# Gated linear attention: one stage written out in place of a loop over heads

## The reference

```python
h = x @ w_in                       # q, k (4 x 256), v, z (4 x 512), a (16)
g = log_sigmoid(a @ w_a2 + b_a) / 16
G = cumsum(g, axis=2)              # within chunks of 64 tokens
G_last = G[:, :, -1:]
q_t = q * 256 ** -0.5 * exp(G)
k_t = k * exp(-G)
k_s = k * exp(G_last - G)
A = where(tril, q_t k_t^T, 0)
o = A v + (what the chunks before left in the state S, through q_t)
o = o * rsqrt(mean(o * o) + eps)   # per head, over its 512 values
y = (o * gn_g * silu(z)) @ w_out
```

## Time and profile before

| what | us |
|---|---|
| median of 3 executions | 1978.28 |
| lowest and highest | 1973.71 and 1978.42 |
| profiled execution, its own time | 1979.1 |
| its span, first to last instruction | 1977.2 |
| mean granted TensorE clock | 0.945 of full |

### The profile page before, as it was taken

One profiled execution on the slowest core, in us unless ns is written; L12 is line 12 of the kernel. 1 busy time (PEld: TensorE's weight loads), 2 busy tenths in 40 slices (PEclk: granted clock), 3 DMA queues, 4 the chain that ended last, 5 costly groups with the idle time before them and its releaser, 6 DMA issues.

```text
span 1977.2 us, 23196 instructions
## 1 busy us (share of the span) xinstructions
PE 1782.6 (90%) x8022; PEld 1466.8 (74%) x8022; DVE 1170.8 (59%) x1681; ACT 597.1 (30%) x1122; POOL 1019.0 (52%) x564
## 2 busy tenths in 40 slices
PE   7799999988999999768898998987779999999967
PEld 6688788766878888656777787766569788887846
DVE  6767433286542544785557565566785956774165
ACT  4354311233212220225313223132222217764031
POOL 5555466645676667446255463643443463333634
PEclk9899999999999999889898999998887999999979
DMA  5222233322333333223122131221221232111311
GB/s 187 70 80 75 86 96 95 96 64 75 95 96 99 99 91 104 69 70 89 51 67 82 53 95 53 85 64 44 64 85 54 65 96 64 54 54 48 99 56 64
DMA packets 47832, 154.89 MB, mean 78 GB/s; under 512 B 6800, under 2 KB 6928, under 8 KB 47632
## 3 DMA queue, kind: packets, MB, share of 16 engines
q1 hardware_dynamic: 46896, 152.35, 25.4%
q10 hardware_dynamic: 864, 1.57, 0.2%
HBM read 151.80 MB, written 2.10 MB: 78 GB/s over the span
## 4 chain that ended last, share of the span: by engine, by line
PE 66%; DVE 17%; ACT 4%; issue 3%; POOL 0%; DVEq 0%; ACTq 0%; POOLq 0%
PE bank L543 22%; PE bank L544 21%; PE bank L545 21%; DVE r L1651 3%; DVE fx L1654 2%; DVE fx L1657 2%; ACT r L1119 2%; DVE eb L1654 1%; DVE h L1657 1%; PE bank L1028 1%; DVE fx L2106 1%; DVE fx L2159 1%; DVE op_lo L1660 1%; PE bank L561 0%; DVE eb L1660 0%
## 5 line engine op out<-in xcount | busy, mean ns | idle before, releaser
L517 POOL TENSOR_SCALAR w_hi<-raw 128x1024 fp32r<-128x1024 f32 (+1 forms) x280 | 309.6, 1106 | 918.1 <-issue 664.3
L519 POOL TENSOR_TENSOR w_lo<-raw,w_hi 128x1024 fp32r<-128x1024 f32 (+1 forms) x280 | 709.3, 2533 | 23.4
L543 PE MATMUL bank<-op_hi,w_hi 128*128 128x512 f32 x1144 | 462.0, 404 | 58.5 <-DVE op_lo L1651 30.5
L544 PE MATMUL bank<-op_lo,w_hi 128*128 128x512 f32 x1144 | 452.8, 396 | 0.0
L545 PE MATMUL bank<-op_hi,w_lo 128*128 128x512 f32 x1144 | 452.1, 395 | 0.0
L543 PE MATMUL bank<-r,w_hi 128*128 128x512 f32 x856 | 346.0, 404 | 41.6 <-DVE r L1651 38.5
L544 PE MATMUL bank<-r,w_hi 128*128 128x512 f32 x856 | 339.1, 396 | 0.0
L545 PE MATMUL bank<-r,w_lo 128*128 128x512 f32 x856 | 339.0, 396 | 0.0
L543 PEld LDWEIGHTS bank<-op_hi,w_hi 128*128 128x128 f32 x1144 | 219.7, 192 | 115.3 <-issue 49.6
L545 PEld LDWEIGHTS bank<-op_hi,w_lo 128*128 128x128 f32 x1144 | 219.1, 192 | 47.1
L544 PEld LDWEIGHTS bank<-op_lo,w_hi 128*128 128x128 f32 x1144 | 219.8, 192 | 44.6 <-issue 1.2
(11 more groups left out here) (206 smaller groups left out, 2342.9 us busy)
## 6 DMA issues: line engine op xcount, KB each, us to landing
raw<-in_weights SPq DMA_DIRECT2D x278, 512.0 KB, 3.6
h<-in_x SPq DMA_DIRECT2D x4, 512.0 KB, 8.3
out<-h SPq DMA_DIRECT2D x1, 2048.0 KB, 7.4
cst<-in_consts SPq DMA_DIRECT2D x1, 1156.5 KB, 11.0
rope_cos<-in_p ACTq DMA_DIRECT2D x3, 256.0 KB, 3.8
rope_sin<-in_p ACTq DMA_DIRECT2D x3, 256.0 KB, 4.1
rope_cos<-in_positions SPq DMA_DIRECT2D x2, 256.0 KB, 11.8
raw<-in_weights SPq DMA_DIRECT2D x4, 128.0 KB, 2.4
```

What stands on the lines that cost most here:

```text
L517: pool.tensor_scalar(hi, raw[:, r, 0:w], 1.0, 0.0, ALU.mult, ALU.add).then_inc(hi_ready, 1)
L519: pool.tensor_tensor(lo, raw[:, r, 0:w], hi.bitcast(F32), ALU.subtract).then_inc(split_ready, 1)
L543: pe.matmul(o, ah, bh, start=start, stop=False, skip_group_check=skip)
L544: pe.matmul(o, ah, bl, start=False, stop=False, skip_group_check=skip)
```

## The change

The loop and `gla_end` become one stage with every instruction written out for each head p. The arithmetic stays. What moves:

- Each engine's work for head p+1 stands between the steps of head p. TensorE makes the four gates of head 0 before its values; q and k of head p+1 ahead of the output of head p; the values and `products(0)` of head p+1 ahead of the projection of head p, and `products(1)` of p+1 right behind it. The second half of head 2's projection stands behind head 3's `osum`.
- The banks change: values, q, k and gates go to banks 0 to 3, the output stays in 4 to 7, and the gated output of blocks 0 to 2 is left in its bank (`gla_tile`) instead of in `h`.
- The log gates `g0` to `g7` and the clearing of `atf` leave the stretch ahead of the stage; VectorE makes the gates between its first steps.
- SyncE loads the weights in the new order (`load_gla`), unit by unit, no longer by the loop.

The core of the diff (TensorE's order, and the waits of four steps):

```diff
-    pe.wait_ge(a.sem, a.at("ab7"))
-    pe.wait_ge(d.sem, d.at("mn7"))
...
-    with pe.Fori(0, GH - 1) as i:
-        gla_head("gla", i, False)
-    gla_head("gla_end", 0, True)
+    def gla_values(c, p):
...
+        for t in range(QT):
+            if c == 0:
+                if p:
+                    pe.wait_ge(a.sem, a.at(f"{('k0', 'q1', 'k1', 'q0')[t]}c_{p}"))
+                if p >= 2:
+                    pe.wait_ge(a.sem, a.at(f"z{t}_{p - 1}"))
...
+    def gla_products(b, p):
+        pe.wait_ge(d.sem, d.at(f"l{b}qj_{p}"))
+        if b == 0:
+            if p == 0:
+                pe.wait_ge(a.sem, a.at("z2_0"))
+            else:
+                pe.wait_ge(d.sem, d.at(f"ol2_{p - 1}"))
...
+    def gla_sum(p):
+        pe.wait_ge(d.sem, d.at(f"oacc2_{p}"))
+        pe.wait_ge(d.sem, d.at(f"on3_{p}"))
+        z.done(full_sum(7), f"osum_{p}")
...
+    for b in GLA_BLOCKS:
+        gla_gate(b, 0)
+    for c in range(4):
+        gla_values(c, 0)
+    gla_products(0, 0)
+    gla_query_key("q0", 1)
+    gla_query_key("k0", 1)
+    gla_query_key("q1", 1)
+    gla_products(1, 0)
+    gla_query_key("k1", 1)
+    gla_values(0, 1)
+    gla_out(0)
+    gla_values(1, 1)
+    gla_sum(0)
+    gla_values(2, 1)
+    gla_values(3, 1)
+    gla_products(0, 1)
+    gla_project(0)
+    gla_products(1, 1)
+    for p in range(1, GH - 1):
+        gla_query_key("q0", p + 1)
+        gla_query_key("k0", p + 1)
+        gla_query_key("q1", p + 1)
+        gla_query_key("k1", p + 1)
+        gla_out(p)
+        gla_gate(3, p)
+        gla_gate(0, p)
+        gla_sum(p)
+        gla_gate(1, p)
+        gla_gate(2, p)
+        gla_values(0, p + 1)
+        gla_values(1, p + 1)
+        gla_products(0, p + 1)
+        gla_values(2, p + 1)
+        gla_values(3, p + 1)
+        gla_project(p, 0, KD if p < GH - 2 else KD // 2)
+        gla_products(1, p + 1)
+    p = GH - 1
+    gla_gate(3, p)
+    gla_gate(0, p)
+    gla_out(p)
+    gla_gate(1, p)
+    gla_sum(p)
+    gla_gate(2, p)
+    gla_project(p - 1, KD // 2, KD)
+    gla_project(p)
```

More of the change, by code:

```diff
@@ L363, in build @@
[L363 to L374, removed]
+              ["zero_y", "zero_at", "al"] + [f"mn{m}" for m in M8], [f"a{m}" for m in range(KD - 1)])
@@ L483, in _, with load_rounds @@
                     load_from(u - 2, u % RAW)
[L484 to L488, removed]
+            def load_rounds(first, rounds):
+                with sp.Fori(first, rounds) as k:
+                    for r in range(RAW):
+                        sp.wait_ge(split_ready, k * RAW + (r - RAW + 1))
+                        load(k * RAW + (r - 2), r)
+            load_rounds(first, gla_first)
+            for u in range(gla_first * RAW, gla_rounds * RAW):
+                sp.wait_ge(split_ready, u - RAW + 1)
+                load_gla(GLA_UNITS[u - U0["gla"]], u % RAW)
+            load_rounds(gla_rounds, rounds)
             for u in range(rounds * RAW, n):
@@ L861, in _ @@
             ath, atl = at_hi.rearrange("p k t -> p (k t)"), at_lo.rearrange("p k t -> p (k t)")
[L863 to L908, removed]
@@ L923, in gla_head @@
[L923 to L929 removed]
+                    z.done(mm, f"o{b}_{p}")
+            def gla_sum(p):
+                pe.wait_ge(d.sem, d.at(f"oacc2_{p}"))
+                pe.wait_ge(d.sem, d.at(f"on3_{p}"))
+                z.done(full_sum(7), f"osum_{p}")
@@ new lines, in gla_project @@
+            def gla_project(p, first=0, end=KD):
+                oh, ol = gla_gated_out(p)
+                for m in range(first, end):
+                    u = gla_unit(f"y{m // 2}_{p}")
+                    if m % 2 == 0:
+                        pe.wait_ge(split_ready, u + 1)
+                    bank = (7, 0, 1, 2)[m % 4]
+                    if m == 0:
+                        pe.wait_ge(a.sem, a.at(f"osqrt_{p}"))
+                        if p == GH - 1:
+                            pe.wait_ge(d.sem, d.at(f"y4_{p - 1}"))
+                    elif m < 4:
+                        if p < GH - 1:
+                            pe.wait_ge(d.sem, d.at(f"vl{bank}_{p + 1}"))
+                        else:
+                            pe.wait_ge(d.sem, d.at(f"y{m + 4}_{p - 1}"))
+                    else:
+                        pe.wait_ge(d.sem, d.at(f"y{m - 4}_{p}"))
+                        if p == GH - 2:
+                            pe.wait_ge(a.sem, a.at(f"osqrt_{p + 1}" if bank == 7 else f"z{bank}_{p + 1}"))
+                    for k in GLA_ORDER:
@@ new lines, in gla_decayed @@
+            def gla_decayed(b, n, p):
+                if p >= GH:
+                    return
+                name = ("qt", "kt", "ks")[n]
+                if n < 2 and p:
+                    sync(a, f"{'qk'[n]}{b}c_{p}")
+                sync(a, f"x{b}{name}_{p}" if n < 2 else f"x{b}s{QT - 1}_{p}")
+                if n:
+                    sync(d, f"l{b}{('qt', 'kt')[n - 1]}_{p}")
+                elif b:
+                    sync(d, f"l0qj_{p}")
+                elif p:
+                    sync(d, f"l1qj_{p - 1}")
+                mul(d, f"m{b}{name}_{p}", tm[:, 0:T], h[:, b if n == 0 else 2 + b], ex[:, 0:T])
@@ L2158, in gla_head @@
-                sync(a, "osqrt", i)
-                d.done(dve.reciprocal(rs, rs), "ors")
-                sync(d, "ors", i)
-                def normalise(b):
-                    mul(d, f"oz{b}", h[:, 4 + b], h[:, 4 + b], rs)
-                normalise(0)
-                for b in range(4):
-                    if b < 3:
-                        normalise(b + 1)
-                    sync(a, f"oh{b}", i)
-                    lo(d, f"ol{b}", go_lo[:, b], h[:, 4 + b], go_hi[:, b])
-                first = 8 if last else 12
```

633 lines of the change are left out of this document (475 added, 158 removed).

## The result

| | before | after |
|---|---|---|
| median, us (4 executions each, same chip) | 1976.48 | 1918.8 |
| lowest and highest | 1973.71 and 1978.42 | 1917.22 and 1921.26 |
| span of the profiled execution | 1977.2 | 1917.0 |
| mean granted TensorE clock | 0.945 | 0.953 |

The ratio of the times is 0.971, 95% interval [0.9692, 0.9728]: 57.7 us faster. The prediction was 1923.

The account below looks back on a forecast made before the run. TensorE, busy 90%, bounds the kernel, so time comes from its idle time and clock. Without waits the stage ends 76.0 us earlier; 17 us of waits and clock plus 3.5 small remain, so 55.5 us gained: 1923, range 1909 to 1944.

Parts of the forecast that it names:

- the case's own 1914 to 1933: The predictor's preferred outcome for the whole kernel: 1923 us, on its own 1914 to 1933, given 43%.
- The signs: In the trace: a 5 to 9 us wait in head 1's values, 0.50 clock behind, none over 2 us before `products`.
- The floor: The stage's matmuls on TensorE, priced at full clock with no waits: 385.5 us.
- The entry, 1.85 us earlier: Stage start: could begin at 903.91 instead of 905.76, since gate 3 of head 0 needs only one bank freed.
- The 12.42, the 7.25 and the 6.37 us: TensorE's waits ahead of head 0's `products(0)`, later heads' `products(1)` (three times) and the last projection; all claimed to go.
- The copy of k1, 7 + 3.5 us: Head 1's first value unit waits for ScalarE's copy: 7 us (bounds 5.7 to 8.8), plus 3.5 of low clock.
- `ol2` ahead of `products(0)` of head 1, 2.5 us: Head 1's `products(0)` waits for a low part of head 0's output: 0 to 5.4 us, taken as 2.5.
- `l1qj` of head 1, 1 us: Head 1's second-half preparation, covered by the 22 us projection against some 24 us of work: a 1 us wait.
- `osum` of heads 1 and 2, 1.5 us each: The sum waits for `on3`, ready at 38.5 to 43.5 us against 40.5: 1.5 us per head, no lowered clock.
- ScalarE's table loads and GpSimd's splitting: Costed at nothing across the stage: 15 table loads instead of 11 (5.1 us), and as many units split by GpSimd.
- the 3.5 for small steps: An allowance of 3.5 us added over the stage for steps too small to place.
- Rival 2: Preparations run beside GpSimd throughout, with longer waits: 39 us left, 37 us gained, 1941 us; 30%.

Follow-up runs that it names:

- e2: Changed kernel with head 1's k1 copy ahead of the exponentials on ScalarE, and head 0's values ahead of the second half's exponentials and first product; 1899.59 us.
- e6: Changed kernel with all eight log gates of head 0 ahead of the first running sum on VectorE, TensorE's order kept; 1922.04 us.
- e5: Changed kernel with `products(1)` of heads 2 and 3 moved ahead of the projection of heads 1 and 2; 1929.73 us.
- e4: Changed kernel with all of head 2's projection ahead of `products(1)` of head 3, none behind the last head's sum of squares; 1924.12 us.
- e3: Changed kernel with the gated output of all four blocks in SBUF, not blocks 0 to 2 in their PSUM banks; 1924.5 us.
- e7: Changed kernel with head 0's values ahead of the second exponentials and their first product, k1's copy left in place; 1910.38 us.

## Why the prediction was right

1923 was said and 1918.8 measured, within the range and within the case's own 1914 to 1933. The signs came too: the one long wait at the place named, 8.96 us within its 5 to 9, released by ScalarE's copy and with a clock of 0.50 behind it, none over 2 us ahead of any `products`, and none for GpSimd. The wait of 2.53 us was on no list. By its steps:

- The floor. 385.5 us at full clock was right: `e2` shows 386.0 of busy time at clock 1.00.
- The entry, 1.85 us earlier. The trace after shows 902.10 for 905.76, 3.66 earlier; 1.93 of this was there before the stage (TensorE's last wait ahead of it ended at 865.28 for 867.21), which leaves 1.73.
- The 12.42, the 7.25 and the 6.37 us go: right, and `e6`, `e5` and `e4` each show which piece of TensorE's work covers them.
- The copy of k1, 7 + 3.5 us. Right in place and releaser, off in both sizes: 8.96 us of wait and 1.8 of clock. The chain, which the prediction counts from the end of `products(1)`, was 17.1 us (973.6 to 990.74), just above its 13.9 to 17. 1.6 of it lay ahead of the first mask copy at 975.20, and no term had that: VectorE was still at the sums that stand ahead of the masks, and the small row of 973.04, 0.17 us at 1081.36, took 2.17 there. 17.1 - 8.2 = 8.9. The clock's 3.5 came from one of three rows. The kernel before has three waits of 7.25 us, and what follows the second and third shows less than the earlier trace rows does for the first:

```profile
1197.10:1201.60 4.50, 4.50 (x18) 4.37 (x19) 0.00 (x0) 1.53 (x3) 0.00 (x0) 0.51 0.02 7
1313.80:1317.60 3.80, 3.76 (x15) 3.63 (x15) 0.00 (x0) 1.60 (x4) 0.00 (x0) 0.50 0.03 9
```

  9.0, 4.5 and 3.8 us at half the clock cost 4.5, 2.2 and 1.9 us. The prediction read the dearest of the three.
- `ol2` ahead of `products(0)` of head 1, 2.5 us: nothing. The last low part ended at 1019.35, 0.9 us before the products. The prediction took the middle of its bounds; the rule on operands in a bank gave the right answer, and `e3` shows it as the cause.
- `l1qj` of head 1, 1 us: nothing (1042.16 against 1045.11).
- `osum` of heads 1 and 2, 1.5 us each: nothing. `on3` of head 1 ended at 1086.41, 2.1 us before the sum at 1088.50. The bound for the sums was taken from rows beside a busy GpSimd; here they ran alone. TensorE made the output from 1069.9 to 1077.6 and finished no weight unit between 1069.9 and 1083, so no slot came free, and GpSimd rested from 1073.8 to 1083.4. VectorE's sums and GpSimd about them, after (the sums answer to the earlier trace rows):

```profile
1078.99 1.22 DVE L2358 TENSOR_TENSOR_SCAN fx<-cst,eb 128x512 f32<-128x512 f32 x1
1080.13 1.20 DVE L2359 TENSOR_TENSOR_SCAN fx<-cst,eb 128x512 f32<-128x512 f32 x1
```

```profile
1071.42 2.39 POOL L603 TENSOR_TENSOR w_lo<-raw,w_hi 128x1024 fp32r<-128x1024 f32 x1
1083.41 1.05 POOL L601 TENSOR_SCALAR w_hi<-raw 128x1024 fp32r<-128x1024 f32 x1 [9.60 <-issue]
```

- The step that was missing: head 0's paragraph has no term for a wait ahead of head 1's q0. I followed the chain of `l0qj` and `l1qj` through head 0, and not the values', which on ScalarE had been put behind two exponentials of half 1. It was 2.53 us of wait and 2.6 at the lower clock; `e7` takes 4.9 of it away.
- ScalarE's table loads and GpSimd's splitting, priced at nothing: right, since nothing waits from 990.80 on. (The trace has 16 loads for 12, not 15 for 11; four more, as priced.)

So the sum came out well partly because errors cancelled: 2.5 + 1 + 3 us of waits were not there, 5.1 us that nobody had asked for were, k1's came out at 10.8 for 10.5, and of the 3.5 for small steps nothing is seen. What is left over 385.5 is 16.4 us, against the 20.5 forecast: 4.1 us less. That the time missed by nearly the same, 4.2, is partly luck, since 1.93 us were gained ahead of the stage and the runs of before scatter by 4.7. Rival 2, preparations beside GpSimd throughout, was right in part: the low parts with both operands in SBUF took 1.33 us on average for 0.69 alone, and k1's wait is its 9 us. But the other preparations ended inside their cover even so, `l1qj` of head 1 with 2.9 us to spare, and the sums ahead of `on3` fell into a pause of GpSimd. `e6` and `e3` show what slow forms cost where the cover is short.

## What to carry to other kernels

When one engine is to be kept busy, list for each of its waits the chain that releases it, and walk every queue in that chain: what costs is an instruction that is ready but stands behind one that isn't (the copy of k1, the values' high part). Undoing such an order moves a few steps in a queue and was worth 4 to 10 us here. Price an operation by what the neighbour engine does at that time, not by its mean, and a pause's cost in clock from every row of its kind, not from one. Where VectorE and GpSimd run side by side, leave one operand in a bank: four operations took 2.6 us so, and 7.8 with both in SBUF.

## What the runs showed of the hardware

- A short wait cost more in clock than a long one. Behind the wait of 2.53 us the granted clock was at 0.50 for 5.6 us, a cost of 2.6 (30.4 us for the 27.8 of `e7`); behind the one of 8.96 us for 3.7, a cost of 1.8. Over the long wait the clock had fallen at 984.3, 2.5 us after TensorE stopped, so that 6.5 us of low clock lay in the wait itself, where they cost nothing:

```profile
951.40:957.00 5.60, 5.59 (x13) 4.48 (x14) 2.63 (x4) 1.80 (x5) 0.00 (x0) 0.50 0.22 84
984.30:990.80 6.50, 0.00 (x1) 0.01 (x1) 4.47 (x9) 4.50 (x11) 0.00 (x0) 0.50 0.23 81
```

  In `e2` a wait of 1.0 us left no mark. In the kernel before, the wait of 12.42 us was followed by 10.1 us at 0.50, and three waits of 7.25 us by 9.0, 4.5 and 3.8. So the length of a wait alone doesn't give its cost in clock here; what does is open.
- An operation of VectorE on 128 x 4 numbers takes 0.17 us alone and took 2.17 at 973.04. GpSimd's row beside it:

```profile
972.02 3.17 POOL L603 TENSOR_TENSOR w_lo<-raw,w_hi 128x1024 fp32r<-128x1024 f32 x1
```

  Both end at 975.2, and GpSimd's took 3.17 us for the 2.4 that it takes where VectorE pauses. The same pair stands at 915.79 and at 943.53: VectorE's small operation ended 0.02 us after GpSimd's in all three. So in these three it was held until GpSimd's operation had ended. Over the stage the groups of VectorE's rows (busy us, mean ns of one) show which forms pay: the low part with both operands in SBUF took 1.33 us on average, the one with an operand in a bank 0.69.

```profile
L1900 DVE TENSOR_TENSOR r<-fx,r 128x512 fp32r<-128x512 f32 x24 | 32.0, 1334 | 39.4 <-ACT r L1274 39.2
...
L1900 DVE TENSOR_TENSOR r<-bank,r 128x512 fp32r<-128x512 f32 x28 | 18.3, 685 | 4.2 <-ACT r L1274 3.7
```

- The written-out program is longer (the page's queue q8, of kind instruction, moved 54 packets for 46), and TensorE showed no wait for it: 313.19 us busy of 313.60.
